# Writing out the head-pair and key-group loops of the first block on four engines

## The chip, the cores and the metric
One core of one Trainium2 chip runs the whole kernel in one launch. The metric is the device time of one execution in microseconds (us). The kernel before takes 4241.44 us, the median of three runs (4240.32 to 4246.13).

## The reference
Two blocks are applied to 256 tokens of width 2048, in float32. The first block has two layers of this kind:

```
h = rmsnorm(x) * (1 + scale) + shift          # scale, shift, gate from c_act @ ada_w
u = h @ w_in                                  # gates, q, k, v of both branches
o_a = gated_delta_rule(l2norm(silu(conv(q))), l2norm(silu(conv(k))), silu(conv(v)), g, beta)   # 16 heads of 128
o_b = swa_with_sinks(rope(q_b), rope(k_b), v_b, sinks)      # 32 query heads over 4 key heads, window 128
y = sigmoid(g_a) * ((rmsnorm(o_a) * silu(z_a)) @ proj_a) + sigmoid(g_b) * ((o_b * silu(z_b)) @ proj_b)
x = x + gate * (y @ w_out)
```

The second block (one layer) is neighborhood attention beside a bidirectional recurrence, a gated feed-forward of width 5632 and a gated embedding. The delta rule solves a unit lower triangular system per chunk of 64 tokens, here by a doubling scheme with levels 2, 4, ..., 64.

## The kernel before
Every weight is read once, in blocks of 128 output columns by 2048 inputs (1 MB). SP loads blocks into the four slots of `raw`. For each half block ScalarE (ACT) copies it to `Wh` in a reduced float format (line 336, the cast), VectorE (DVE) makes the rest `Wl` (line 342), and TensorE (PE) runs three matmuls for each of eight input tiles, `Wh*Hh`, `Wh*Hl`, `Wl*Hh` (`pe_half`, lines 271 to 273). A half block is 24 matmuls. ACT copies the finished tile out of the accumulator bank, or DVE does.

The order is written out by hand for each engine, and the engines wait for one another on semaphores. `half_used` is counted up by PE at the end of each half block and lets the next cast start; `hi_ready` leads from the cast to DVE; `lo_ready` leads from DVE to PE and, for the refill of `raw`, to SP; `tile_taken` tells that a bank is free. A class `Steps` gives each stage one semaphore per engine, and a wait for a named step is a wait for `run * steps + place` (line 121).

In each of the two layers the delta rule runs over 8 pairs of heads, one pair being 8 blocks, thus 16 half blocks. The code is a pipeline of two stages over pairs. `pe_gdn`, `act_gdn`, `dve_gdn` and `pool_gdn` take the pair number `i` and two flags: with `fresh` the projections, the convolution and the norms of pair `i` are made, with `chain` the triangular solve, the state and the output of pair `i-1` are worked in between the same half blocks. Pair 0 is written out (`fresh` alone), pairs 1 to 7 run in a loop `Fori(1, PAIRS)` on the engine itself, and 8 (`chain` alone) is written out again. Sliding-window attention has the same shape over 4 key heads (`pe_swa`, `act_swa`, `dve_swa`): `g = 0` is written out, 1 to 3 are the loop `Fori(1, KV)`, 4 is written out.

In such a loop `i` lives in a register. Wait values and some addresses are worked out from it by small register instructions in each engine's own instruction stream: `S.wait` at line 121, the cast's wait at line 335, the weights of the convolution at line 1122 (`par(l, "conv", i * 24 + m * 4 + t, 1)`, one column for each of 24 operations of a pair), and others. At the end of an iteration there is a compare and a branch (recorded at the loop's line: 2373 GpSimd, 2395 and 2400 PE, 2420 and 2426 ACT, 2451 and 2458 DVE).

Places to which the text below comes back, with `n` the half block within a pair:

- `conv(m)`, lines 1119 and 1122: one multiply and three multiply-adds on DVE, each waiting for the one before.
- Line 1144 (DVE, `before(10)`): `vn`, which PE needs at line 911 for the output of the second chunk (`middle(10)`).
- Line 1008 (ACT, `work(11)`): the square of the output, which PE sums at line 966 (`middle(11)`).
- Line 1135 (DVE): the masked block of level 2, which PE needs at line 952 (`middle(2)`).
- Line 1448 (ACT): the last query tile of a key group, which PE needs at line 1398 for the rotary turn.
- The feed-forward loop of the second block, line 2200, and the loops at 1261 and 2286, are device loops in both versions, as are all loops of SP.

Of the kernel before, what the change touches and what calls it, by code (L numbers as in the profile page):

```python
# [31 lines left out]
PAIRS = HEADS // 2  # L32
KV = 4
# [90 lines left out]
def build_program(nc, places, x_t, c_t, pos, stream, ada, ple_w, ple_x, rg_w, rpb, consts, params, params2, out_t, until=None):  # L124
    ctx = ExitStack()
    with ctx:
# [45 lines left out]
        def ws(at, *shape, of=WS):  # L172
            n = int(np.prod(shape))
            v = of[:, at:at + n]
            if len(shape) == 2:
                v = v.rearrange("p (a b) -> p a b", b=shape[1])
            if len(shape) == 3:
                v = v.rearrange("p (a b c) -> p a b c", b=shape[1], c=shape[2])
            return v
# [23 lines left out]
        def seed(eng, who):  # L203
            for S in stages:
                S.seed(eng, who)
# [114 lines left out]
        def pe_spin(pe, count):  # L320

            for _ in range(count):
                pe.matmul(B[5][:, 0:T], ones, C[:, 0:T], start=True, stop=True)
# [312 lines left out]
        def pe_ada(pe, third):  # L636

            S = st_ada
            pe.wait_ge(const_in, 80)
            pe.wait_ge(ada_used, third * KT + KT)  # L640
            for j in range(KT):
                i = pe.matmul(B[1][:, third * KT + j:third * KT + j + 1], ada_acc[third][:, j * P:(j + 1) * P], ones[:, 0:1], start=True, stop=True)
            S.done(i, "pe", f"sums{third}")
# [424 lines left out]
        def pool_gdn(pool, l, i, fresh, chain):  # L1068

            def pause():  # L1070
                pool.tensor_tensor(SEC_X[0:1, 0:1], ident[0:1, 0:1], ident[0:1, 0:1], ALU.subtract)

            S, F = st_gdn, st_fr
            if chain:
                S.start("pool")
                r = l * PAIRS + (i - 1)
                S.wait_runs(pool, "dve", r)
                S.done(pool.tensor_tensor(Zz[:], mask4("ident"), mask4("ident"), ALU.subtract), "pool", "z2")
                for s in (4, 8, 16, 32, 64):
                    S.wait(pool, "pe", f"MZ{s // 2}", r)  # L1080
                    S.done(pool.tensor_tensor(Zz[:], mask4("ident"), mask4("ident"), ALU.subtract), "pool", f"z{s}")
            if fresh:
                F.start("pool")
                f = l * PAIRS + i
                if not chain:
                    st_pre.wait(pool, "act", "tok_exp", l)
                F.wait(pool, "dma", "gb", f)
                pause()
                rows = [gb[:, 0].rearrange("p h (t c) -> p (h t) c", c=P), gb[:, 1].rearrange("p h (t c) -> p (h t) c", c=P)]
                e = [u4(E[:, n, :]) for n in range(3)]  # L1090
                for n, (a, b, m) in enumerate(((rows[0], tok(1, i), "m_low"), (tok(0, i), rows[1], "m_up"), (tok(0, i), rows[0], "m_upd"))):
                    if chain and n == 1:
                        S.wait(pool, "pe", "Z64", r)
                        pause()
                    if chain and n == 2:
                        S.wait(pool, "pe", "o_second", r)
                        pause()
                    F.done(pool.tensor_tensor(e[n], a, b, ALU.subtract), "pool", f"e{n}")
                    F.wait(pool, "pool", f"e{n}", f)
                    F.done(pool.tensor_tensor(e[n], e[n], mask4(m), ALU.add), "pool", f"E{n}")  # L1100
# [666 lines left out]
        def pool_na(pool, i):  # L1767

            S = st_na
            S.start("pool")  # L1770
            for h in range(4):
                S.wait(pool, "dma", f"bias{h}", i)
                v = bias[h % 2].rearrange("p a (r c) -> p (a r) c", c=64)
                S.done(pool.tensor_tensor(v, v, const("near").unsqueeze(1).to_broadcast([P, 8, 64]), ALU.add), "pool", f"bias{h}")
# [593 lines left out]
        @block.gpsimd  # L2368
        def _(pool):
            seed(pool, "pool")  # L2370
            for l in range(LAYERS):
                pool_gdn(pool, l, 0, True, False)
                with pool.Fori(1, PAIRS) as i:
                    pool_gdn(pool, l, i, True, True)
                pool_gdn(pool, l, PAIRS, False, True)
            with pool.Fori(0, 2) as i:
                pool_na(pool, i)
            st_zero.start("pool")
            st_n[2].wait(pool, "dve", f"lo{KT - 1}")
            for g in range(4):  # L2380
                st_zero.done(pool.tensor_tensor(ws(g * 1024, 8, P, of=Yf), ident.unsqueeze(1).to_broadcast([P, 8, P]), ident.unsqueeze(1).to_broadcast([P, 8, P]), ALU.subtract), "pool", f"zero{g}")

        @block.tensor
        def _(pe):
            seed(pe, "pe")
            pe_ada(pe, 0)
            for g in range(4):
                pe_stat(pe, 0, g, sq_of[:, 4 * g:4 * g + 4, :])
            pe_ada(pe, 1)
            pe_spin(pe, 11)  # L2390
            for l in range(LAYERS):
                pe_pre(pe, l)
                pe_gdn(pe, l, 0, True, False)
                pe_spin(pe, 9)
                with pe.Fori(1, PAIRS) as i:
                    pe_gdn(pe, l, i, True, True)
                pe_gdn(pe, l, PAIRS, False, True)
                pe_end(pe, l, 0)
                pe_swa(pe, l, 0, False)
                with pe.Fori(1, KV) as g:  # L2400
                    pe_swa(pe, l, g, True)
                pe_end(pe, l, 1, pe_swa(pe, l, KV, True))
                pe_out(pe, l)
            pe_second(pe)

        @block.scalar
        def _(act):

            act.sem_inc(tile_taken, 2)
            act_setup(act)  # L2410
            act.wait_ge(x_in, 16)
            act_stat(act, 0, first=True)
            for n in range(4):
                act.wait_ge(landed[n // 2], 16)
                act.copy(Wh[:, n, :], raw[:, n // 2, (n % 2) * (D // 2):(n % 2 + 1) * (D // 2)]).then_inc(hi_ready, 1)
            for l in range(LAYERS):
                act_mod_norm(act, l)
                act_pre(act, l)
                act_gdn(act, l, 0, True, False)
                with act.Fori(1, PAIRS) as i:  # L2420
                    act_gdn(act, l, i, True, True)
                act_gdn(act, l, PAIRS, False, True)
                act_end(act, l, 0)
                st_gm.wait(act, "pe", "sums", l)
                act_swa(act, l, 0, False)
                with act.Fori(1, KV) as g:
                    act_swa(act, l, g, True)
                act_swa(act, l, KV, True)
                act_end(act, l, 1)
                act_out(act, l)  # L2430
                if l == 0:
                    act_stat(act, l + 1)
            act_second(act)

        @block.vector
        def _(dve):
            seed(dve, "dve")
            dve_setup(dve)
            dve_ada(dve, 0)
            dve_ada(dve, 1)  # L2440
            st_ada.wait(dve, "pe", "sums1")
            dve_mod(dve, 0)
            dve_nw(dve, 0, 0)
            for n in range(4):
                dve.wait_ge(hi_ready, n + 1)
                dve.tensor_tensor(Wl[:, n, :], raw[:, n // 2, (n % 2) * (D // 2):(n % 2 + 1) * (D // 2)], Wh[:, n, :].bitcast(F32), ALU.subtract).then_inc(lo_ready, 1)
            for l in range(LAYERS):
                dve_mod_norm(dve, l)
                dve_pre(dve, l)
                dve_gdn(dve, l, 0, True, False)  # L2450
                with dve.Fori(1, PAIRS) as i:
                    dve_gdn(dve, l, i, True, True)
                dve_gdn(dve, l, PAIRS, False, True)
                st_gdn.wait(dve, "dve", "o_lo", l * PAIRS + PAIRS - 1)
                dve_end(dve, l, 0)
                dve_gate(dve, l)
                dve_swa(dve, l, 0, False)
                with dve.Fori(1, KV) as g:
                    dve_swa(dve, l, g, True)
                dve_swa(dve, l, KV, True)  # L2460
                st_swa.wait(dve, "dve", "lo3", l * KV + KV - 1)
                dve_end(dve, l, 1)
                dve_out(dve, l)
            dve_second(dve)
# [145 lines left out]
```

## Time and profile before

| | |
|---|---|
| median of the runs | 4241.44 us |
| the profiled execution | 4242.38 us, its span 4240.5 us |
| PE busy | 95% of the span, 30878 matmuls |
| DVE, ACT, GpSimd busy | 65%, 45%, 6% |
| granted TensorE clock, mean | 0.987 |
| chain that ended last | PE 77%, DVE 8%, ACT 7%, issue 6%, DMA 1% |
| DMA | 724.38 MB, 171 GB/s on the mean |
| instruction packets | 164 on queue 8, 48 on queue 14 |

The span is the time from the first to the last instruction; 1.9 us of the execution lie outside of it. PE is the matmul array, PEld its weight loads, a q behind an engine's name its instruction sequencer. Matmuls overlap: one recorded as 0.28 us starts 0.12 us after the one before it.

### The profile page before, as it was taken

How to read it: one execution, taken by the hardware profiler on the slowest of the kernel's cores; microseconds unless marked ns; L12 is line 12 of the kernel's file. 1: busy time of each engine (PE TensorE's matmuls, PEld its weight loads, DVE VectorE, ACT ScalarE, POOL GpSimd, SP SyncE). 2: the span in 40 equal slices, each digit the busy share in tenths (PEclk: the TensorE clock that was granted, in tenths of full speed). 3: DMA queues.
4: the chain of work that ended last, by engine and by line, in shares of the span. 5: the costliest groups of instructions: out<-in, count | busy, mean ns of one | idle time of the engine just before them, and what ended most of it. 6: DMA issues, size and time to landing. Idle time of an engine off the chain costs nothing.

```text
span 4240.5 us, 78225 instructions
## 1 busy us (share of the span) xinstructions
PE 4036.8 (95%) x30878; PEld 3846.5 (91%) x30878; DVE 2759.2 (65%) x3689; ACT 1909.5 (45%) x2772; POOL 267.3 (6%) x252
## 2 busy tenths in 40 slices
PE   2999999999999999999999999999888999999998
PEld 2999999999999999999999999999887888888888
DVE  7667777566678766677756576565466656565665
ACT  1443435334544344353533454454365544444465
POOL 0012121000000001212100000000000000000000
PEclk8999999999999999999999999999999999999999
DMA  9433333574358833333357434543443354555543
GB/s 392 154 130 118 132 115 128 206 272 154 140 191 315 298 136 123 120 133 119 130 192 278 160 138 149 182 176 133 168 146 114 137 189 179 179 179 185 179 143 120
DMA packets 114132, 724.38 MB, mean 171 GB/s; under 512 B 12608, under 2 KB 13056, under 8 KB 36224
## 3 DMA queue, kind: packets, MB, share of 16 engines
q1 hardware_dynamic: 88416, 639.17, 41.9%
q10 hardware_dynamic: 25504, 82.13, 5.4%
q8 instruction: 164, 2.69, 0.2%
q14 instruction: 48, 0.39, 0.0%
HBM read 719.09 MB, written 2.16 MB: 170 GB/s over the span
## 4 chain that ended last, share of the span: by engine, by line
PE 77%; DVE 8%; ACT 7%; issue 6%; DMA 1%; DVEq 0%; ACTq 0%; SPq 0%
PE bank L271 15%; PE bank L273 15%; PE bank L272 15%; PE bank L288 9%; PE bank L289 4%; ACT Wh L336 3%; PE bank L952 2%; PE bank L956 2%; PE bank L931 2%; DVE Wl L342 2%; DMA raw<-in_ada 1%; PE bank L2116 1%; PE bank L2118 1%; PE bank L2117 1%; PE bank L314 1%
## 5 line engine op out<-in xcount | busy, mean ns | idle before, releaser
L336 ACT CAST Wh<-raw 128x1024 fp32r<-128x1024 f32 x1140 | 1189.9, 1048 | 2020.8 <-PE bank L273 1509.8
L342 DVE TENSOR_TENSOR Wl<-raw,Wh 128x1024 fp32r<-128x1024 f32 x1140 | 1417.4, 1246 | 1002.0 <-ACT Wh L336 997.1
L271 PE MATMUL bank<-H,Wh 128*128 128x256 f32 x5536 | 1618.6, 292 | 0.5 <-ACT WS L1987 0.4
L272 PE MATMUL bank<-H,Wh 128*128 128x256 f32 x5536 | 1567.9, 283 | 0.0
L273 PE MATMUL bank<-H,Wl 128*128 128x256 f32 x5536 | 1567.2, 283 | 0.0
L271 PEld LDWEIGHTS bank<-H,Wh 128*128 128x128 f32 x5536 | 1063.0, 192 | 18.2 <-issue 17.4
L272 PEld LDWEIGHTS bank<-H,Wh 128*128 128x128 f32 x5536 | 1063.8, 192 | 9.2 <-issue 8.6
L273 PEld LDWEIGHTS bank<-H,Wl 128*128 128x128 f32 x5536 | 1062.2, 192 | 0.0
L288 PE MATMUL bank<-H,Wh 128*128 128x512 f32 x1600 | 561.9, 397 | 10.9 <-ACT WS L2170 5.6
L289 PE MATMUL bank<-H,Wl 128*128 128x256 f32 x1600 | 446.9, 279 | 0.0
L288 PEld LDWEIGHTS bank<-H,Wh 128*128 128x128 f32 x1600 | 300.3, 188 | 84.7 <-ACT WS L2170 6.2
L289 PEld LDWEIGHTS bank<-H,Wl 128*128 128x128 f32 x1600 | 301.5, 188 | 0.0
L271 PE MATMUL bank<-O,Wh 128*128 128x256 f32 x896 | 256.7, 286 | 5.7 <-DVE Y L1323 2.9
L273 PE MATMUL bank<-O,Wl 128*128 128x256 f32 x896 | 255.9, 286 | 0.0
L272 PE MATMUL bank<-O,Wh 128*128 128x256 f32 x896 | 255.8, 286 | 0.0
L2116 PE MATMUL bank<-O,Wh 128*128 128x256 f32 x704 | 201.2, 286 | 5.6 <-ACT WS L2170 4.3
L2117 PE MATMUL bank<-O,Wh 128*128 128x256 f32 x704 | 199.1, 283 | 0.0
L2118 PE MATMUL bank<-O,Wl 128*128 128x256 f32 x704 | 199.0, 283 | 0.0
L271 PEld LDWEIGHTS bank<-O,Wh 128*128 128x128 f32 x896 | 174.7, 195 | 6.4 <-DVE Wl L342 6.2
L272 PEld LDWEIGHTS bank<-O,Wh 128*128 128x128 f32 x896 | 174.5, 195 | 0.0
L273 PEld LDWEIGHTS bank<-O,Wl 128*128 128x128 f32 x896 | 174.3, 195 | 0.0
L2116 PEld LDWEIGHTS bank<-O,Wh 128*128 128x128 f32 x704 | 134.8, 191 | 10.2 <-ACT WS L2170 6.3
(374 smaller groups left out, 4947.9 us busy)
## 6 DMA issues: line engine op xcount, KB each, us to landing
raw<-in_stream SPq DMA_DIRECT2D x572, 1024.0 KB, 4.8
WS<-in_ada ACTq DMA_DIRECT2D x94, 512.0 KB, 6.6
raw<-in_ada SPq DMA_DIRECT2D x32, 1024.0 KB, 7.5
gm_more<-in_ada ACTq DMA_DIRECT2D x20, 512.0 KB, 6.9
WS<-rows_d ACTq DMA_DIRECT2D x16, 512.0 KB, 4.8
KR<-in_ada ACTq DMA_DIRECT2D x14, 512.0 KB, 6.8
X<-in_x_t SPq DMA_DIRECT2D x1, 2048.0 KB, 17.4
WS<-in_rpb ACTq DMA_DIRECT2D x8, 256.0 KB, 2.9
```

The costliest lines, as they stand in the source:

```text
L271: pe.matmul(out[:, 0:T], wh, xh[:, kt, :], start=first, stop=False)
L272: pe.matmul(out[:, 0:T], wh, xl[:, kt, :], start=False, stop=False)
L273: mm = pe.matmul(out[:, 0:T], wl, xh[:, kt, :], start=False, stop=last)
L288: pe.matmul(out[:, :], wh, x[:, kt, :, :], start=kt == 0, stop=False)
L289: mm = pe.matmul(out[:, 0:T], wl, x[:, kt, 0, :], start=False, stop=kt == KT - 1)
L336: act.copy(Wh[:, n % 4, :], raw[:, (sbk + 2) % 4, k * (D // 2):(k + 1) * (D // 2)]).then_inc(hi_ready, 1)
L342: dve.tensor_tensor(Wl[:, n % 4, :], raw[:, (sbk + 2) % 4, k * (D // 2):(k + 1) * (D // 2)], Wh[:, n % 4, :].bitcast(F32), ALU.subtract).t ...
L931: m = pe.matmul(B[0][:, u * 64:(u + 1) * 64], u4(E[:, 1, :])[:, u, :], upper(Mm[:, u:u + 1, :], s)[:, 0], start=True, stop=True)
L952: m = pe.matmul(B[1][:, u * 64:(u + 1) * 64], Zz[:, u, :], upper(Mt[:, u:u + 1, :], s, 1)[:, 0], start=True, stop=True)
L2116: pe.matmul(o, wh, ah, start=x == 0, stop=False)
L2117: pe.matmul(o, wh, al, start=False, stop=False)
L2118: m = pe.matmul(o, wl, ah, start=False, stop=x == 3)
```

## The change
The loops over pairs (on four engines) and over key groups (on three) in the first block's layers become Python loops: each iteration has instructions of its own, with numbers in place of registers. What is computed, and its order on each engine, stays. As `for l in range(LAYERS)` was a Python loop before, this makes 2 x 7 copies of the pair body and 2 x 3 of the group body where there were 2 and 2.

```diff
@@ gpsimd
-                with pool.Fori(1, PAIRS) as i:
+                for i in range(1, PAIRS):
                     pool_gdn(pool, l, i, True, True)
@@ tensor
-                with pe.Fori(1, PAIRS) as i:
+                for i in range(1, PAIRS):
                     pe_gdn(pe, l, i, True, True)
...
-                with pe.Fori(1, KV) as g:
+                for g in range(1, KV):
                     pe_swa(pe, l, g, True)
@@ scalar
-                with act.Fori(1, PAIRS) as i:
+                for i in range(1, PAIRS):
                     act_gdn(act, l, i, True, True)
...
-                with act.Fori(1, KV) as g:
+                for g in range(1, KV):
                     act_swa(act, l, g, True)
@@ vector
-                with dve.Fori(1, PAIRS) as i:
+                for i in range(1, PAIRS):
                     dve_gdn(dve, l, i, True, True)
...
-                with dve.Fori(1, KV) as g:
+                for g in range(1, KV):
                     dve_swa(dve, l, g, True)
```

## Rows read from the trace of the kernel before

**Rows 1.** The page: the chain by engine, and the first instruction queue.
```profile
PE 77%; DVE 8%; ACT 7%; issue 6%; DMA 1%; DVEq 0%; ACTq 0%; SPq 0%
...
q8 instruction: 164, 2.69, 0.2%
```

**Rows 2.** Busy time by window: pair 2 (in the loop), pair 8 (written out).
```profile
core 0: us, PE busy (x) PEld busy (x) DVE busy (x) ACT busy (x) POOL busy (x), PEclk, DMA share, GB/s
298.80:370.50 71.70, 70.69 (x584) 68.63 (x583) 51.48 (x80) 32.03 (x42) 15.39 (x15) 1.00 0.36 124
729.20:798.10 68.90, 67.32 (x566) 66.18 (x564) 36.41 (x54) 26.02 (x34) 6.25 (x6) 1.00 0.35 125
```

**Rows 3.** Waits of the weight loads: waited for, us in total, times, longest.
```profile
PEld bank L952 <- DVE WS L1135: 12.4, 14, 0.9
...
PEld bank L1398 <- ACT WS L1448: 9.3, 8, 1.7
...
PEld bank L966 <- ACT WS L1008: 6.5, 16, 0.5
...
PEld bank L911 <- DVE WS L1144: 4.7, 14, 0.3
```

**Rows 4.** Single lines, the loops' branches: count, ns min/median/max, first and last start.
```profile
L2395 PEldq COMPARE_BRANCH  x14: 83/215/243, 294.4 to 2111.1; - x14
...
L2451 DVEq COMPARE_BRANCH  x14: 50/56/67, 298.9 to 2115.5; - x14
...
L2200 PEldq COMPARE_BRANCH  x5: 83/3717/3801, 3518.5 to 4078.7; - x5
```

**Rows 5.** DMA queues (packets, MB), 300 to 728 us: all but queue 1.
```profile
q10 hardware_dynamic: 1632, 3.15, 2.5%
```

**Rows 6.** DMA queues, 729 to 790 us (pair 8): the instruction queues.
```profile
q8 instruction: 4, 0.07, 0.4%
q14 instruction: 1, 0.01, 0.0%
```

**Rows 7.** DVE timeline, convolution and what follows: loop, then pair 0.
```profile
346.21 1.75 DVE L1122 SCALAR_TENSOR_TENSOR gm_more<-Y,PAR,gm_more 128x256 f32<-128x256 f32 x3
347.88 0.41 DVE L1144 TENSOR_TENSOR WS<-WS,bank 128x256 f32<-128x256 f32 x1
...
215.48 1.53 DVE L1122 SCALAR_TENSOR_TENSOR Y<-Y,PAR 128x256 f32<-128x256 f32 x3
```

**Rows 8.** PE timeline around line 911: loop, then pair 8.
```profile
347.93 0.28 PE L273 MATMUL bank<-H,Wl 128*128 128x256 f32 x1
...
348.67 0.28 PE L912 MATMUL bank<-WS 128*128 128x128 f32 x1
...
778.24 0.28 PE L273 MATMUL bank<-H,Wl 128*128 128x256 f32 x1
...
778.58 0.28 PE L912 MATMUL bank<-WS 128*128 128x128 f32 x1
```

**Rows 9.** PE timeline at line 966: loop, then pair 8.
```profile
352.58 0.70 PE L966 MATMUL bank<-WS,C 128*128 128x512 f32 x1 [0.19 <-ACT WS L1008]
...
782.54 0.70 PE L966 MATMUL bank<-WS,C 128*128 128x512 f32 x1 [0.25 <-ACT WS L1008]
```

**Rows 10.** Timelines of ACT, DVE, PE on the way to line 952.
```profile
288.03 1.05 ACT L336 CAST Wh<-raw 128x1024 fp32r<-128x1024 f32 x1 [0.52 <-PE bank L273]
...
297.48 1.23 DVE L342 TENSOR_TENSOR Wl<-raw,Wh 128x1024 fp32r<-128x1024 f32 x1 [1.31 <-ACT Wh L336]
...
307.56 0.42 DVE L1135 TENSOR_TENSOR WS<-bank,C 128x256 f32<-128x256 f32 x1
...
308.04 0.44 PE L952 MATMUL bank<-WS 128*128 128x64 f32 x2 [0.69 <-DVE WS L1135]
```

**Rows 11.** PE timeline at line 1398, in the group loop.
```profile
1049.12 0.70 PE L1398 MATMUL bank<-WS,C 128*128 128x512 f32 x1 [0.75 <-ACT WS L1448]
```

**Rows 12.** PE timeline at the back edge of the feed-forward loop.
```profile
3522.49 0.49 PE L288 MATMUL bank<-H,Wh 128*128 128x512 f32 x1 [1.80 <-ACT WS L2170]
```

## The prediction

> **What bounds the kernel now.** I read the page first. The chain that ended last is PE for 77% of the span [rows 1], so an edit to the instruction streams counts only where PE is idle, or where something that PE waits for moves. Next the busy time by window, because this edit touches two stretches of each layer. A pair in the loop takes 71.70 us, of which PE is busy 70.69 [rows 2], at a granted clock of 1.00. All that any change of the other engines can give back there is 1.01 us a pair. The list of waits says what this idle time is: in the two layers PE waits 14 times at line 952 for DVE (12.4 us in weight-load idle time), 16 times at 966 for ACT, 14 times at 911 for DVE (4.7 us), and 8 times at 1398 for ACT [rows 3]. None of these waits ends on a branch, a register or a DMA. The branches themselves I read line by line [rows 4].
>
> **The change part by part.**
>
> *The branches go.* Of the 14 records at PE's pair loop 12 are taken (7 iterations a layer, the last falls through), and the four of the group loop make 16. One takes 0.215 us [rows 4], 16 x 0.215 = 3.4 us of sequencer time. The first starts at 294.4 us, while the array reaches that edge only at about 298.6 us, where DVE's branch also stands at 298.9 [rows 4]: the sequencer is some 4.2 us ahead, and the array works through what is queued. DVE's branch takes 0.056 us, behind a queued operation. I take 0; the bounds are 0 and the 3.4 us.
>
> *Instruction loading.* Within the seven loop iterations of layer 0 no instruction packet moves at all: beside the weights' queue 1 there is only queue 10 [rows 5]. The body stays on the core. In pair 8, which is written out, 4 packets of 16 KB and 1 of 8 KB come in 61 us [rows 6], so a written-out pair of 71.7 us takes 4.7 of the large ones. 12 more pairs are 56 packets, 4 more groups of 60 us at the same rate 16: some 72 on queue 8, so 164 [rows 1] becomes about 236, and the small ones grow by about 20. That is 1.2 MB beside 724 MB. Does it delay PE? Pair 8 has line 966's wait as in the loop but for 0.06 us, explained below, and its 911 passes without a wait [rows 8, 9], so crossing these blocks cost the array nothing there. I take 0. The weights don't suffer either: a 1 MB block is needed each 71.7 / 8 = 9.0 us, lands 4.8 us after its issue, and no wait of the casts in these stretches ends on a DMA. If that cover were gone, a late 16 KB packet on one of 16 rings could hold a block by about a microsecond.
>
> *Register operations of the convolution go: a gain.* In the loop three multiply-adds take 1.75 us from first start to last end, in pair 0, written out, 1.53 [rows 7]. Each is 0.485 us long in both, so from the first to the last start it is 1.26 against 1.04 us; with the hand-over of the multiply ahead of them (0.49 us to the next start against 0.39) a convolution of four ends 0.32 us earlier. Six a pair give DVE 1.9 us back, which matters only where PE waits for what follows: line 1144 comes right behind one of them (347.88 + 0.41 = 348.29 us), and PE starts line 911 at 348.34, 0.41 us after line 273 where 0.12 is normal. From 273 to the first 912 the loop needs 348.67 - 347.93 = 0.74 us, pair 8 needs 778.58 - 778.24 = 0.34 [rows 8]. The upper bound is this 0.40 us. But the convolution starts behind DVE's low part, which follows a cast, and the cast will be 0.055 us later (next part). So `vn` comes 0.32 - 0.055 = 0.27 us earlier, and its weight load, now 0.41 us behind the undisturbed pitch, is still 0.14 behind. I take 0.27 us for each of the 14 waits: -3.8 us. The bounds are 0 and 14 x 0.40 = 5.6 us.
>
> *The cast starts later: a loss.* In the loop a register operation takes up one of the cast's two waits (the landing of the weights), and the cast itself holds the other, on `half_used`. In written-out code one of the two becomes a separate semaphore instruction of the sequencer, and the cast is dispatched only behind it. The trace prices it. Line 966 waits for a square that follows a cast without a gap; PE is idle 0.19 us before it in the loop, 0.25 in pair 8 [rows 9]: 0.055 us unrounded. Three waits hang on such a cast:
> - Line 966, pairs 1 to 7, 14 times: +0.8 us. Pair 8's two pay it already.
> - Line 952, pairs 2 to 8, 14 times. Its cast starts at 288.03 us released by PE [rows 10]; from there ACT is busy without a hole through ten operations to the casts at 296.4, DVE takes over at 297.48 released by the cast, and is busy without a hole to 307.56 + 0.42, where PE has waited 0.69 us [rows 10]. The whole 20 us lies end to end, nothing in it shortens (none of it is a convolution), and a later start passes through: +0.8 us. If a slack of 0.06 us hides in it, 0.
> - Line 1398, groups 1 to 3, 6 times, idle 0.75 us [rows 11], behind the cast and the copy of 1448: +0.3 us.
>
> Together +1.9 us; bounds 0 and double that, if other waits are dispatched late as well.
>
> *The rest.* SP's stream is unchanged. GpSimd is busy 15.39 us of a pair [rows 2], and no wait of PE names it. DVE and ACT lose about as many register instructions as they have operations, all of it beside a full array.
>
> Sum: -3.8 + 1.9 = -1.9 us. The profiled execution, 4242.4 us, goes to 4240.5; the median of the runs, 0.9 us lower than it, from 4241.4 to **4239.5 us**.
>
> **A rule against this sum.** The Trainium skill ("Runtime: NRT & Kernel Launch", section "Instruction fetch mechanics") says that a taken branch whose target isn't in the two blocks now held forces a fetch before execution goes on, and that kernels prefer full unrolling for this. The body of a pair, 4.7 blocks, is well beyond two. The trace disagrees for it [rows 4, 5]: no packets and 0.215 us. It agrees for the feed-forward loop. The page also gives PE room for 2048 instructions, eight blocks, and by that figure both observations fit.
>
> **The rivals.**
>
> *A. Back edges stall PE, so their removal pays.* For it: the feed-forward loop's taken branch lasts 3.72 us, and the array is idle 1.80 us behind it, or at least beside it, as ACT is named too [rows 4, 12]. 16 edges at 1.80 are 29 us: 4212 us. It is the rule above as a mechanism of this kernel. Against it: no packets and no idle PE at the pair loop's edge. Chance 4 in 100.
>
> *B. Written-out ACT and DVE code stalls at block boundaries: slower.* Both stretches that lead to line 952 have no slack, and ACT and DVE queue only a few instructions, so a block that comes late there goes through to PE. Of some 20 new small blocks about a third (20 of 71.7 us, with more instructions to the microsecond than elsewhere) fall into them: 7 x 3.7 us, the only fetch seen whole [rows 4], is 26 us: 4267 us. It decides as soon as a block is asked for less than 3.7 us before it is needed. Against it: pair 0 and pair 8 cross such blocks [rows 6] and show none of it. Chance 6 in 100.
>
> *C. The feed-forward loop lands worse in its blocks: slightly slower.* Its code is moved by all that is inserted ahead. After its back edge PE has no lead. The fetch of the target's block already costs 1.80 us [rows 12]; where the target sits in the last fifth of a block, the next block is missed too, up to about 1.9 us more at each of 4 taken edges: +7.5 us, with the sum above 4247 us. The odds of the fifth are its chance, 14 in 100 with what speaks for a smaller effect. The loops at 1261 and 2286 need fewer blocks than a pair's 4.7 or little more, and I expect them to stay resident.
>
> *D. Nothing is seen*, as gain and loss cancel or both are covered by something unseen: 4241.4 us. I count it with the forecast.
>
> **How the numbers follow.** Forecast with D 76 in 100, A 4, B 6, C 14. A measurement of this kernel tells about 0.2% (8.5 us) from no change. The forecast and nearly all of C are within that; C passes it only with the losses at their upper bound, 1 in 100. Faster by more: A and 2 of the forecast's 76, where the branches' bound (3.4) adds to the full gain of 5.6. Slower: B, C's 1, and 1 for late dispatch elsewhere. That gives 6, 86 and 8. The range reaches from the bounds' best, 4241.4 - 5.6 - some of the branches, 4234 us, to C's end, 4248 us; A and B, 10 in 100, stay outside.
>
> **What would show it.** In the profile after: no branch records at lines 2373 to 2458 but for what stays; queue 8 at 225 to 245 packets; three multiply-adds at 1.53 us in every pair; from 273 to 912 around line 911 0.4 to 0.5 us instead of 0.74; idle before 966 0.25, before 952 0.74, before 1398 0.80 us; a pair at 71.5 us. A pair under 70.7 or over 72 us makes the working wrong, as does a feed-forward back edge that moves by over a microsecond (C) or a new wait for "issue" on ACT or DVE (B).

## The result and the profile after

The changed kernel takes 4257.9 us in the median of ten runs (4252.1 to 4265.0). The kernel before, run beside it, takes 4243.9 (4240.3 to 4250.4). The ratio is 1.0031, 95% interval 1.0022 to 1.0041: slower by 13 us, with 9 to 17 inside the interval. The prediction was 4239.5 us in a range of 4234 to 4248, and 8 in 100 for slower. It was wrong.

The profiled executions have spans of 4240.5 and 4261.8 us. The page after, the rows that answer to [rows 1]:

```profile
PE 79%; DVE 9%; ACT 8%; issue 3%; DMA 1%; ACTq 0%; DVEq 0%; SPq 0%
...
q8 instruction: 238, 3.90, 0.4%
```

The 238 packets are within the 225 to 245 expected. Next, the stretches that were edited. First a pair that is in the loop before (line 919 of one pair to line 919 of the next), then its counterpart after, both from the view of busy time by window, columns as in [rows 2]:

```profile
368.20:439.94 71.74, 70.73 (x585) 68.67 (x584) 51.50 (x79) 32.04 (x44) 15.39 (x15) 1.00 0.36 124
```
```profile
370.46:441.96 71.50, 70.50 (x584) 68.59 (x583) 51.79 (x79) 32.04 (x43) 15.49 (x15) 1.00 0.37 125
```

A pair is 0.22 to 0.24 us shorter. The four waits, in the list of waits after, against [rows 3]:

```profile
PEld bank L952 <- DVE WS L1135: 13.2, 14, 0.9
...
PEld bank L1398 <- ACT WS L1448: 9.6, 8, 1.7
...
PEld bank L966 <- ACT WS L1008: 7.3, 16, 0.5
```

Line 911 has left the list, where it had 4.7 us. The other three have grown, by 0.8, 0.3 and 0.8 us. PE's timeline after, against [rows 8 to 11]:

```profile
350.41 0.28 PE L273 MATMUL bank<-H,Wl 128*128 128x256 f32 x1
350.55 0.49 PE L911 MATMUL bank<-Y 128*128 128x128 f32 x2
350.88 0.39 PE L912 MATMUL bank<-WS 128*128 128x128 f32 x2
...
354.84 0.70 PE L966 MATMUL bank<-WS,C 128*128 128x512 f32 x1 [0.25 <-ACT WS L1008]
...
310.52 0.66 PE L952 MATMUL bank<-WS 128*128 128x64 f32 x4 [0.74 <-DVE WS L1135]
...
1048.87 1.55 PE L1398 MATMUL bank<-WS,C 128*128 128x512 f32 x3 [0.81 <-ACT WS L1448]
```

From 273 to 912 it is 0.47 us now, 0.74 before. The idle times are 0.25, 0.74 and 0.81, where the prediction had 0.25, 0.74 and 0.80. So the edited stretches did what was forecast: the feed-forward part begins at 3423.75 us after and 3427.11 before, 3.4 us earlier.

The loss is behind that, in a part that the diff doesn't touch. The whole feed-forward part, from the first matmul of line 2116 to the first of 2150, before and after:

```profile
3427.10:4108.80 681.70, 666.73 (x4430) 608.47 (x4428) 417.37 (x430) 320.61 (x390) 0.00 (x0) 1.00 0.51 180
```
```profile
3423.75:4130.90 707.15, 676.98 (x4430) 615.67 (x4428) 417.35 (x430) 320.60 (x390) 0.00 (x0) 0.98 0.49 174
```

It takes 25.5 us more: PE is idle for 30.2 us instead of 15.0 (+15.2), and busy 10.3 us longer with the same 4430 matmuls. The sum of the case is -3.35 + 25.45 - 0.85 (the tail behind it) = +21.25, the difference of the spans. This execution lies near the upper end of its runs; if the other two terms hold in the median run too, its 13 us mean that the feed-forward part costs some 17 there.

The idle time is that of the loop's four back edges. The branch's record after, and PE's timeline behind the first edge, against [rows 4, 12]:

```profile
L2200 PEldq COMPARE_BRANCH  x5: 83/5082/5303, 3515.1 to 4100.8; - x5
```
```profile
3520.73 0.49 PE L288 MATMUL bank<-H,Wh 128*128 128x512 f32 x1 [3.39 <-issue]
3521.06 0.28 PE L289 MATMUL bank<-H,Wl 128*128 128x256 f32 x1
3521.18 0.40 PE L288 MATMUL bank<-H,Wh 128*128 128x512 f32 x1
3521.42 0.28 PE L289 MATMUL bank<-H,Wl 128*128 128x256 f32 x1
3521.54 0.40 PE L288 MATMUL bank<-H,Wh 128*128 128x512 f32 x1
3525.91 0.37 PE L289 MATMUL bank<-H,Wl 128*128 128x256 f32 x1 [3.97 <-issue]
```

Here are two stalls where there was one of 1.80 us: 3.39 us behind the branch, then five matmuls, then 3.97 us. Over the four edges the first kind is 3.39, 3.17, 2.09 and 3.28 us, the second 3.97, 1.81, 1.58 and 3.08, 22.4 us together; before, it was 1.80, 1.90, 1.53 and 1.88, 7.1 us. The difference, 15.3 us, is all of the idle time added. At this edge both stalls end on "issue": no other engine is late. (Where the view names ACT or DVE before such an idle time, as in [rows 12], the branch's record shows what held PE all the same.)

The rest is the clock. Busy time by window around the same edge after (PEclk is the third column from the end):

```profile
3520.00:3523.00 3.00, 1.21 (x5) 0.91 (x6) 0.28 (x1) 0.00 (x0) 0.00 (x0) 0.82 0.70 246
3523.00:3526.00 3.00, 0.09 (x1) 0.09 (x1) 0.00 (x0) 0.00 (x0) 0.00 (x0) 0.50 0.35 139
3526.00:3530.00 4.00, 4.00 (x17) 3.42 (x17) 0.00 (x0) 0.75 (x1) 0.00 (x0) 0.66 0.02 4
3530.00:3533.00 3.00, 3.00 (x19) 2.63 (x18) 1.22 (x1) 1.23 (x2) 0.00 (x0) 1.00 0.00 0
```

The granted clock goes to 0.50, its lower level of 1.2 GHz, with the idle time and is still there when PE works again: 17 matmuls in 4 us, where 19 take 3 us at the full 2.4 GHz. It is at the lower level for 6.8, 6.8, 3.4 and 10.2 us at the four edges, 27.3 us in all, and nowhere in this part before. PE is busy for 17.8 of these 27.3 us (the second stalls take up much of the rest). Work at half speed takes twice as long, so 8.9 us of the added 10.3 are the clock's; the last 1.4 us have no row of their own.

What comes over the instruction queue fits. DMA by queue, before, from 3513 to 3517 us, ahead of the branch (3518.5 us), and then from 3519 to 3526, behind it:

```profile
q8 instruction: 1, 0.02, 2.3%
...
q8 instruction: 2, 0.03, 1.7%
```

And after, in the four microseconds from 3514 to 3518 us, around the branch (3515.1 us):

```profile
q1 hardware_dynamic: 166, 1.23, 84.1%
q8 instruction: 2, 0.03, 5.7%
```

Before, one 16 KB packet starts 3.9 us ahead of the branch and is in before it. It is the next block in sequence, which a taken branch doesn't need. The target's block is asked for 1.3 us behind the branch and takes 0.9 us. After, both start together, 1.15 and 1.31 us behind the branch, and take 1.66 and 1.98 us.

### The profile page after: what moved, and what is told of

It reads as the page before. It is cut to its first block, busy times and chain, and to the rows that moved or that the text cites. A ratio compares the mean times of both kernels' runs of the same rounds, so it can differ in the third digit from the quotient of the medians.

```text
span 4261.8 us, 74893 instructions
## 1 busy us (share of the span) xinstructions
PE 4042.3 (95%) x30878; PEld 3850.2 (90%) x30878; DVE 2762.7 (65%) x3689; ACT 1908.6 (45%) x2772; POOL 268.7 (6%) x252
## 4 chain that ended last, share of the span: by engine, by line
PE 79%; DVE 9%; ACT 8%; issue 3%; DMA 1%; ACTq 0%; DVEq 0%; SPq 0%
PE bank L271 16%; PE bank L272 15%; PE bank L273 15%; PE bank L288 9%; PE bank L289 4%; ACT Wh L336 3%; DVE Wl L342 2%; PE bank L952 2%; PE bank L956 2%; PE bank L931 2%; DMA raw<-in_ada 1%; PE bank L2116 1%; PE bank L2118 1%; PE bank L2117 1%; PE bank L314 1%
## 5 line engine op out<-in xcount | busy, mean ns | idle before, releaser
L288 PE MATMUL bank<-H,Wh 128*128 128x512 f32 x1600 | 574.7, 403 | 15.5 <-DVE Wl L342 6.4
L289 PE MATMUL bank<-H,Wl 128*128 128x256 f32 x1600 | 453.3, 283 | 10.4 <-issue 10.4
```

Source lines behind the costliest of these rows:

```text
L288: pe.matmul(out[:, :], wh, x[:, kt, :, :], start=kt == 0, stop=False)
L289: mm = pe.matmul(out[:, 0:T], wl, x[:, kt, 0, :], start=False, stop=kt == KT - 1)
```

## The experiments

A "place" is an instruction's position within a block of 16 KB. The Trainium skill ("Advanced Engine Details and Errata", section "ISA Cache") gives such a block 256 instructions. The runs agree where the place is set. The directive of e5 to e7 and e10 puts the loop's set-up instruction at its place, and the target of the branch stands one behind it. With place 240 (e7), 15 instructions are left in the target's block, and at the first edge 15 records of PE's stream come before the second stall: two register operations, seven weight loads and six matmuls.

In the expectations, the place was counted in the built program where no directive sets it. That count is off, and the traces give better ones. In e5 the directive fills up with 14 idle instructions to reach place 0:

```profile
L2201 PEldq NOP  x14: 13/13/13, 3382.2 to 3383.2; - x14
```

So after's target stands at 243, with 13 instructions left (two register operations, six loads and five matmuls come before its second stall), and e1's at 72. For the kernel before, take the fetch of the second block behind the target's: from the moment when the array works again, it starts 103 to 105 matmuls later at all four edges, as in e5 (104 to 105), while with place 128 (e6) it is 41 to 45. The target of before is thus near place 0, not at 74, and e2's near 171 (an estimate from these counts): there the fetch starts after 23 to 27 matmuls.

Sums of idle time (behind the four edges), the time at the lower clock and the length are of the feed-forward part of each profiled execution; the ratio is to the kernel before on the same chip:

```
kernel                    part us  idle us  at 1.2 GHz  branches us         ratio
before                      681.7      7.1         0.0  3.5 to 3.8
after                       707.2     22.4        27.3  5.3 5.1 4.0 5.2     1.0031
e1 after + 85               682.6      6.5         3.4  3.5 to 3.7          0.9997
e2 before + 171             693.2     12.4        10.2  4.7 to 5.2          1.0030
e3 DVE alone                685.5      7.0         6.8  3.4 to 3.9          0.9980
e4 ACT alone                683.9      7.0         3.4  3.6 to 3.8          1.0007
e5 after, place 0           681.8      6.5         3.4  3.4 to 3.7          0.9987
e6 after, place 128         681.9      6.5         0.0  3.4 to 3.8          0.9982
e7 before, place 240        701.3     18.5        20.5  5.2 3.8 5.0 3.6     1.0041
e8 DVE, FF out, pair order  716.4        -        20.5  none                1.0073
e9 DVE, FF out              677.5        -         0.0  none                0.9969
e10 DVE alone, place 128    686.2      7.6         3.4  3.6 to 4.1          0.9985
```

**e1, the after kernel with its code moved by 85 instructions.** The increments stand at the start of PE's program, before any work, on a semaphore that nothing waits for.

```diff
+        pad_sem = sem("pad")
...
+            for _ in range(85):
+                pe.sem_inc(pad_sem, 1)
```

> The changed kernel with 85 further semaphore increments at the start of PE's stream (where PE waits some 85 us for VectorE), which move the feed-forward loop's first instruction on PE from place 245 to place 74 of a 256-instruction block, as in the kernel before. Theory P (the loss is only the place of that loop in its blocks): back-edge branch 3.7 us, idle about 1.8 us behind it and none a few matmuls later, no drop of the granted clock there, and the time 5 us under the kernel before (what the written-out pairs gained ahead of the feed-forward part), 4239 us. Rival S (longer code and its loading slow the second block whatever the place): 4258 us, as the changed kernel.

4242.59 us, ratio 0.9997 [0.9988, 1.0006]. 85 instructions that compute nothing take the whole loss away. There is no second stall, and the branches are those of before:

```profile
L2201 PEldq COMPARE_BRANCH  x5: 83/3486/3690, 3513.8 to 4074.9; - x5
```

**e2, the kernel before with its code moved by 171.**

```diff
+        pad_sem = sem("pad")
...
+            for _ in range(171):
+                pe.sem_inc(pad_sem, 1)
```

> The kernel before, all loops kept, with 171 semaphore increments at the start of PE's stream, which move the feed-forward loop's target from place 74 to place 245. Theory P: the two stalls at each of 4 back edges (about 3.3 and 3 us instead of 1.8 us), the clock at half for about 7 us after each, and the time about 19 us over the kernel before, 4263 us. Rival S: 4244 us, as nothing is written out.

4257.0 us, ratio 1.003 [1.0019, 1.0041]: the loss of the change, without the change.

```profile
L2201 PEldq COMPARE_BRANCH  x5: 83/4978/5238, 3518.8 to 4090.6; - x5
```

The branches are as long as after's and again two packets start nearly together, 0.6 to 1.3 us behind the branch. The second stall is missing, and in this the expectation missed: the target isn't where it is in after but near place 171, with some 85 instructions left in its block. That makes the run of use, since it shows the long branch by itself: 12.4 - 7.1 = 5.3 us of idle time, and 10.2 us at the lower clock, make the part 11.5 us longer.

**e3 and e4, one engine's loops alone.** VectorE's in the first run, ScalarE's in the second:

```diff
-                with dve.Fori(1, PAIRS) as i:
+                for i in range(1, PAIRS):
                     dve_gdn(dve, l, i, True, True)
...
-                with dve.Fori(1, KV) as g:
+                for g in range(1, KV):
                     dve_swa(dve, l, g, True)
```

> The kernel before with the two kinds of loops written out on VectorE alone. PE's stream is the same, so its feed-forward loop stays at place 74. Theory: line 911's wait goes (0.40 us less for each of 14), lines 966, 952 and 1398 keep 0.19, 0.69 and 0.75 us of idle time as ScalarE keeps its loop: 5.6 us under the kernel before, 4238 us. Rival (the gain at 911 comes from PE's own register instructions): 911 keeps 0.41 us and the time stays at 4244 us.

> The kernel before with the loops written out on ScalarE alone. Theory: every cast released by PE starts 0.055 us later, idle before 966 0.25 us, before 952 0.74 us, before 1398 0.80 us, line 911 stays late or is 0.05 us later still: 2 to 3 us over the kernel before, 4246 us. Rival (the later start comes with PE's written-out waits): these stay at 0.19, 0.69, 0.75 us, and the time at 4244 us.

VectorE alone: 4235.5 us, ratio 0.998 [0.9971, 0.9989]. ScalarE alone: 4245.5 us, 1.0007 [0.9998, 1.0016]. PE's timeline of VectorE alone and then of ScalarE alone, at lines 911 and 966:

```profile
348.59 0.28 PE L273 MATMUL bank<-H,Wl 128*128 128x256 f32 x1
348.70 0.45 PE L911 MATMUL bank<-Y 128*128 128x128 f32 x2
348.99 0.39 PE L912 MATMUL bank<-WS 128*128 128x128 f32 x2
...
352.89 1.12 PE L966 MATMUL bank<-WS,C 128*128 128x512 f32 x2 [0.20 <-ACT WS L1008]
```
```profile
283.38 1.12 PE L966 MATMUL bank<-WS,C 128*128 128x512 f32 x2 [0.25 <-ACT WS L1008]
...
350.97 0.49 PE L911 MATMUL bank<-Y 128*128 128x128 f32 x2 [0.18 <-DVE WS L1144]
```

The gain comes from VectorE alone and the loss from ScalarE alone. (ScalarE's run time by itself doesn't show a loss, as its interval holds 1; the timeline does.) With VectorE's loops out, 273 to 912 is 0.40 us instead of 0.74, 911 follows 273 at the undisturbed pitch, and 966 stays at 0.20; a pair is 0.39 us shorter, 5.5 us over 14, near the prediction's upper bound for this term. (0.05 us of the 0.39 are two further waits of PE for VectorE at line 952, 28 and 34 us into the pair, which the prediction didn't list.) With ScalarE's out, 966 has its 0.25, 911 waits longer than before, and a pair is 0.13 us longer.

**e5 and e6, the feed-forward loop's target at place 0 and 128, in the after kernel.** The directive moves the loop once, ahead of it: in e5 by 14 idle instructions, in e6, e7 and e10 by a jump (one branch record at the directive's line).

```diff
         def feed_forward(eng, gu, hidden, dn):
...
+            if gu is pe_gu:
+                eng.addr_align(256, offset=0, max_nops=32)
             with eng.Fori(0, (FF_GROUPS - 1) // 2) as i:
```

> The changed kernel with a directive ahead of PE's feed-forward loop that puts its first instructions at place 0 of a 256-instruction block. So the target's block has some 250 instructions left, and the branch, 1875 instructions on, stands about 85 behind a block's start. Theory P in two parts: a second stall comes only where few instructions are left behind the target (none here), and the branch itself takes 5 instead of 3.7 us where it stands shortly behind a block's start, as the load of the block after it is then in flight (here). So one stall of about 3.2 us at each of 4 edges, as in the run with 171 increments, 4250 us. Rival: the long first stall too comes from the few instructions left behind the target; then 3.7 us branches and 4238 us.

> The same with place 128: about 125 instructions left behind the target, the branch some 213 behind a block's start. Theory P: branches of 3.7 us, stalls of 1.5 to 1.9 us, no second stall, the clock not lowered there by more than a slice or two, 4239 us. Rival S (length of the code): 4258 us.

Place 0: 4239.2 us, ratio 0.9987 [0.9978, 0.9996]. My expectation missed. The loop has 1876 instructions on PE, so its branch stands at place 84 of its block, and I expected the fetch of the next block to be still on the way there. It is in: it starts 3.9 us ahead of the branch, as in the kernel before, whose loop stands at nearly the same place. In place of the expected 5 us:

```profile
L2202 PEldq COMPARE_BRANCH  x5: 83/3497/3725, 3522.4 to 4082.8; - x5
```

The time is the one that this expectation's rival had, but its mechanism, few instructions left behind the target, is out: e2 has long branches at all four edges with some 85 left. No run moves the branch without the target, as the loop's length is the same in all. What ties the long branch to the fetch of the next block is the packets: at each of the nine branches of 4.7 us and more (three in after, four in e2, two in e7) that fetch starts 0.6 to 1.3 us behind the branch, and at none of the others.

Place 128: 4236.1 us, 0.9982 [0.9973, 0.9991], as expected. With its loop in a harmless place the written-out kernel is faster than the kernel before: by 7.6 us at place 128 (3.8 to 11.5 by the interval) and 5.5 at place 0 (1.7 to 9.3). The profile's count of the gain in front of the feed-forward part is 3.4 us, inside the second interval and just under the first.

**e7, the target at place 240, in the kernel before.** The same directive, offset 240.

> The kernel before, all loops kept, with PE's feed-forward loop put at place 240: about 14 instructions left behind the target, the branch some 70 behind a block's start. Theory P: both stalls, as in the changed kernel (3.3 us and 2 to 4 us at each edge, then half the clock for 3 to 10 us), 20 us over the kernel before, 4263 us. Rival (the second stall needs the long code of the changed kernel): one stall, 4255 us or less.

4261.9 us, ratio 1.0041 [1.0028, 1.0054], where 4263 was expected. PE's timeline at the first edge:

```profile
3524.19 0.49 PE L288 MATMUL bank<-H,Wh 128*128 128x512 f32 x1 [3.32 <-DVE Wl L342]
3528.85 0.59 PE L288 MATMUL bank<-H,Wh 128*128 128x512 f32 x1 [3.06 <-issue]
```

Both stalls are there in a kernel with every loop kept, with 15 instructions left in the target's block; the second comes at every edge (1.7 to 3.1 us). Only two of the four branches are long (5.2 and 5.0 us). At the short ones the two fetches do not start together: the next block's starts 0.3 and 2.8 us ahead of the branch, the target's 1.15 and 1.21 us behind it.

**e8 and e9, without back edges.** VectorE's loops as above, and the feed-forward loop written out on PE.

```diff
-            with eng.Fori(0, (FF_GROUPS - 1) // 2) as i:
+            out = gu is pe_gu
+            for i in range((FF_GROUPS - 1) // 2) if out else [None]:
+              with nullcontext(i) if out else eng.Fori(0, (FF_GROUPS - 1) // 2) as i:
```

> The kernel before with the pair and group loops written out on VectorE alone, and the feed-forward loop written out on PE alone, so that the back edge whose target isn't held is gone. Theory: line 911's wait goes (-5.6 us) and the four stalls of 1.8 us go (-7.1 us): 4231 us, and the time of a run scatters less. Rival: PE waits there for ScalarE's tile at line 2170, which the waits name, and little of the 7 us comes back: 4238 us.

4274.3 us, ratio 1.0073 [1.006, 1.0085]: a miss, for a reason of mine. `pe_gu` asks `isinstance(run, int)` and then works two blocks as a pair (`pe_pair`), which it does only ahead of the loop; with the loop written out every `run` is an int, and PE takes that order in all eleven groups. PE's waits in this part:

```profile
PEld bank L288 <- DVE Wl L342: 24.1, 9, 2.7
PEld bank L310 <- ACT WS L2170: 11.2, 9, 1.2
```

The pair order needs its low parts sooner than VectorE makes them. The run tells of that order, not of the branches, and so it was made again:

```diff
-            pair = isinstance(run, int)
+            pair = isinstance(run, int) and run == 0
```

> The loops of the first block written out on VectorE alone, and the feed-forward loop written out on TensorE, this time with the order of work that the loop has (the helper takes its pair order only for the group ahead of the loop). My theory, that a back edge costs what its fetch of code leaves uncovered: no COMPARE_BRANCH of line 2200 on TensorE and none of the four idle times ahead of line 288 (7.1 us in all in the kernel before), none of the new waits L314 to L288 of the run before, no slice at the half clock in the feed-forward part, and about 4229 us, some 7 below the run with VectorE's loops alone (4235.5). Rival 1: straight code pays the same fetches as it runs (each of the four iterations passes some 7 blocks of code), so the 7 us come back as stalls spread over the part: about 4235.5. Rival 2: with the back edges gone the part is set by VectorE's and ScalarE's casts, which then are late: a gain of 2 to 4 us only, with waits of TensorE on Wl in the place of the stalls.

4231.3 us, ratio 0.9969 [0.9959, 0.9979], the fastest version here. By the ratios it is 4.7 us under VectorE alone, but the two intervals overlap, so that difference rests on the profiles (parts of 677.5 and 685.5 us, one execution each). Its feed-forward part:

```profile
3416.30:4093.80 677.50, 667.82 (x4430) 609.64 (x4428) 417.36 (x430) 320.87 (x390) 0.00 (x0) 1.00 0.50 181
```

PE is idle for 9.7 us instead of 15.0: of the 7.1 us of the edges some 1.8 come back, since PE now waits 7.5 us at line 2116, for ACT and DVE, where it was 5.6. That is a part of the second rival, the smaller one. The first, that straight code pays the same fetches, is out. The instruction queue in this part, in the kernel before and then in this one:

```profile
q8 instruction: 43, 0.70, 0.4%
```
```profile
q8 instruction: 35, 0.57, 0.3%
```

35 packets are 5 passes of 7.3 blocks; the loop needs 43, two more at each of its four edges, the block that isn't needed and the target's. So the loop kept nothing for the next pass, and writing it out costs no fetch more.

**e10, VectorE alone with place 128.** The diffs of the two runs together.

> The loops written out on VectorE alone, all loops kept on TensorE, and the feed-forward loop's target put at place 128 of a block on TensorE. My theory: the back edges already cost what a well-placed one costs (branches 3.4 to 3.9 us, idle 1.5 to 1.9 us), so a place changes nothing more: 4235 us, within 2 of the run with VectorE's loops alone (4235.5), ratio to before 0.998. Rival: the place 128 is itself worth some 3 us, since the written-out kernel ran at 4236.1 with it and at 4239.2 with place 0: then about 4232.

4237.5 us, ratio 0.9985 [0.9976, 0.9994] against 0.998 without the directive. A good place shows no gain over one that is already harmless.

## Why the prediction was wrong

*The branches go.* Taken as 0, and right: all that a pair gains is in the waits at 911, 952 and 966 (next point). One reading behind it was wrong. The new iteration's first work on the array is line 919, at 296.47 us, not what runs at 298.6. So the sequencer is 2.0 us ahead and not 4.2, which still covers a branch of 0.215 us.

*Register operations and the cast.* From 273 to 911 it was to fall by 0.27 us and fell by 0.28 (0.413 to 0.138); 966 was to rise by 0.055 and rose by 0.058, 952 by 0.055 and rose by 0.055, 1398 by 0.055 and rose by 0.056. A pair was to gain 0.16 and gained 0.22 to 0.24. The rest is at line 952 again: from one 919 to the next PE starts the same 583 matmuls before and after, and in their median starts the difference moves by +0.06 us at the first 952, by -0.03 and -0.02 at two later ones (28 and 34 us into the pair), by -0.28 at 911 and +0.05 at 966, -0.23 in all. VectorE alone has the same two steps, so they belong to its loops. Ahead of the feed-forward part the gain is 3.4 us where the sum had 1.9. VectorE alone and ScalarE alone show that the two terms are what I took them for: a pair changes by -0.39 and by +0.13 alone, -0.26 as a sum, and by -0.22 to -0.24 together.

*Instruction loading: I take 0.* Right for the stretches written out: 74 packets more and no stall at 911, 952, 966 or 1398. Rival B is out: in the whole layer ACT and DVE wait for no block in a way that reaches PE. Rival A is out too: e1 removes the same 16 edges and gains nothing like 29 us.

*The step that failed is the sizing of rival C*, "the next block is missed too, up to about 1.9 us more at each of 4 taken edges: +7.5 us", and with it its chance of 14 in 100 and the sentence that nearly all of C is within 0.2%. The mechanism was right for one of its two parts. The measured price of an edge in after is 22.4 / 4 = 5.6 us of idle time instead of 1.8, so +3.8 us and not +1.9, in two terms. The first, the longer branch, I did not have at all (+4.8 us over the four edges). When the next block's fetch starts together with the target's, the later of the two lands 3.0 to 3.4 us behind the branch, where a target's fetch lands 1.8 to 2.8 us behind a short one, and the array is idle for 2.8 to 3.4 us. The second is the one that I had, the block behind the target's: 1.6 to 4.0 us an edge, 10.4 us in all. Then the clock: the prediction has no term for it, and PE's busy time grows by 10.3 us in after's profiled execution, by 6.3 in e2 and by 8.3 in e7. Together that is 25.5 us in this execution, some 17 in the median run, where rival C had 7.5.

The chance was too low for the same reason. I counted one bad fifth of a block, for the target. There are two conditions, on the target's place and on the branch's, and e2 shows that the second one alone costs 0.3%. The two coincide in after. With the branch at place 70 (after) it is long in three of four passes, at 68 (e7) in two; at 84 (e5) and 212 (e6) in none. In e2 it stands near the boundary of two blocks and is long in all four. If it holds from a block's start up to there, 71 to 84 of 256 places are bad, an estimate of 28 to 33 in 100 where the prediction had 14, and the 11.5 us of e2 are beyond 0.2%.

The rule of the Trainium skill that the prediction weighed ("Runtime: NRT & Kernel Launch", "Instruction fetch mechanics") is right for the feed-forward loop (its target is fetched at each edge) and wrong for the pair loop (no packet, 0.215 us a branch [rows 4, 5]). The prediction added that a room of eight blocks on PE fits both. Place 0 tells against it as a sufficient reason: there the loop's 1876 instructions lie within eight blocks, and the edge still fetches its target.

*What stays open.* That the next block in sequence, fetched ahead of the branch, displaces the loop's first block would explain place 0; it was not tried with a shorter loop. Why the target's block takes longer when two start together isn't settled. From 1 to 3 us behind the branch the weights' queue is busy for 56 to 71% before and 56 to 78% after, so at like load the pair takes longer, which speaks for the two fetches hindering each other. But a single fetch of 1.87 us with a branch of 4.1 us occurs too (e10, first edge, the queue at 79%). And the share of the clock is read from profiles, not from a run that held it fixed: time at the lower level of 3.4 to 6.8 us occurs at harmless edges too (e1, e3 to e5, e10), with 1 to 4 us more of busy time, and varies from one execution to the next.

## What to carry to other kernels

An edit that inserts or removes code moves every later loop in its blocks. Look for a loop whose taken branch takes microseconds in the profile, and put its target at a set place before the edit is judged: here the same edit is 0.3% slower, or with the loop at a harmless place equal to 0.2% faster (0.9997, 0.9987 and 0.9982, intervals that overlap). And write out what the trace shows to be late, not all that can be written out: VectorE's loops alone give the whole gain, and the one loop that pays for its back edges is another one, which nobody had touched. When a loop is written out, ask of every helper whether it behaves otherwise for a constant index.

## What the runs showed of the hardware that was not expected

- A taken branch to a block that isn't held costs 3.3 to 4.1 us of the sequencer and 1.4 to 2.2 us of an array that had 2.2 us queued. It costs 4.7 to 5.3 us of the sequencer and 2.8 to 3.4 us of the array where the fetch of the next block in sequence starts together with the target's, 0.6 to 1.3 us behind the branch. With the branch at place 84 the next block is in before it.
- With 13 or 15 instructions left in the target's block a second stall of 1.6 to 4.0 us follows (after, e7); with the loop put at 0 or 128, or some 85 instructions left (e2), there is none.
- Idle times of 3.4 and 4.0 us with five matmuls between them go with a granted clock of 0.50 that outlasts them by 2.9 us (after, first edge); single ones of about 3 us (e2) are followed by 3.4 us of it, three times of four.
- A loop of 1876 instructions on PE is fetched anew in every pass (43 packets against 35 straight), while the pair loop runs without a packet [rows 5].
